# Compression of cached pages: copies of the next unit ahead of the second half's sums and activation, and the prompt units' turning split between the halves of layer 1

## The chip, the core and the metric

The kernel runs on one core of a Trainium2 chip. The metric is the device time of one execution in microseconds. TensorE does matmuls and transposes and writes them to PSUM; VectorE (DVE), ScalarE (ACT) and GpSimd (POOL) work element by element; SyncE (SP) and GpSimd issue the DMAs here. Each engine works through its own queue in order, and engines wait for each other by semaphores (`wait_ge`, `then_inc`).

## The reference, cut to what matters

One step of a hybrid decoder layer for a prompt of 1024 tokens and 8 sequences of the decode group with 2048 cached tokens each. The change touches only the compression of K and V of the compressed branch, which is done for the prompt (its new K and V rows) and for each decode sequence (its cached pages):

```python
def _compress(kraw, w1, b1, w2, b2, pe):
    ...
    ch = kp.reshape(B, n_ch, CMP_STRIDE, NSA_KV_HEADS, HEAD_DIM)
    w1r = w1.reshape(CMP_RATIO, CMP_STRIDE, HEAD_DIM, CMP_HIDDEN)
    parts = jnp.einsum('bnsgd,rsdh->rbngh', ch, w1r)
    n_cmp = n_ch - CMP_RATIO + 1
    h = parts[0, :, 0:n_cmp]
    for r in range(1, CMP_RATIO):
        h = h + parts[r, :, r:r + n_cmp]
    h = h + (pe.reshape(-1) @ w1) + b1
    out = jax.nn.gelu(h) @ w2 + b2
```

`CMP_STRIDE` is 16, `CMP_RATIO` 2, `HEAD_DIM` 64 with 2 KV heads, `CMP_HIDDEN` 256: a chunk of 16 rows goes through a layer of 256 hidden values with its neighbour, then through the activation and a second layer to 64.

## The kernel before

`compress_and_decode` holds the stage. Its work is cut into **units**, ten of them: unit 0 is the prompt's K, units 1 to 4 are K of two decode sequences each, unit 5 is the prompt's V, units 6 to 9 V of two sequences each. `units` has (which of K and V, pair, items); an **item** is one sequence's pages (or the prompt). `FIRST = (0, 5)` are the prompt units, with one item; all others have two.

TensorE runs, in its program order: the turning of unit 0, and then for each unit u the turning of unit u+1 (`transposes`), layer 1 of unit u (`layer1`), layer 2 of unit u-1 (`layer2`), and the second step of a set of ada rows (`late_back`). Turning a decode item is 16 transposes in four groups, each group into one PSUM bank; three banks rotate (`bank_free`: a group waits until the group three before it is copied). The prompt item has two groups. Layer 1 runs in two halves of 128 hidden values (`hh`), each into a bank of its own, for a decode unit with four sets of matmuls (L1114, L1116, L1121, L1123), since the chunks' halves are combined by sums and differences; for a prompt unit with 16 products (L1111). Ahead of one half of a decode unit stand 8 products for the ada vectors of a later stage (`late_rows`, L1081).

The other engines:

- `read_chunks` (L1209) copies the transposed groups out of PSUM into X, even groups on ScalarE, odd ones on VectorE, four instructions a group. X has two buffers, so copies of unit u wait for layer 1 of unit u-2.
- ScalarE: after the copies of the last item of unit u+1 it runs `gelu(u)`: for each half it waits for layer 1's half, copies the `middle` out of PSUM (L1261), perhaps the ada row (L1267), waits until VectorE has summed the half (`summed`) and applies the activation (L1270). Only then come the copies of unit u+2.
- VectorE: after the copies of the last item of unit u it forms the differences of both items (`first_difference`, L1304 to L1309), then `sums` of both halves of unit u-1 (L1328 to L1331, for a prompt unit L1321 and L1322), `late` (L1355: the ada addition, which waits for TensorE's `late_back`) and `out(u-2)` (L1342 or L1347: the result of layer 2).
- GpSimd: for each item it waits for the item's last transposes, loads the item that is four further on into the same of four raw buffers (L1011), and then forms another difference (`later_difference`, L1021), which waits for the item's copies.

A second half of layer 1 of unit u waits for `summed` of unit u-1's second half, and layer 2 of unit u-1 for its activation.

Of the kernel before, what the change touches and what calls it, by code (L numbers as in the profile page):

```python
# [18 lines left out]
ACT = mybir.ActivationFunctionType  # L19
# [589 lines left out]
FIRST = 4  # L609
# [261 lines left out]
def compress_and_decode(nc, a, o, m, PS, sem):  # L871
# [41 lines left out]
    with ExitStack() as st:  # L913
# [158 lines left out]
        def _(pe):  # L1072
# [18 lines left out]
            def layer1(u):  # L1091
# [9 lines left out]
                pe.wait_ge(pe_ready, which + 1)  # L1101
                for hh in range(2):
                    col = slice(P * hh, P * hh + P)
                    if u in late_at and hh == late_half(u):
                        late_rows(late_at.index(u))
                    if u:
# [56 lines left out]
                transposes(pe, items[k])  # L1163
            for u in range(NU):
                if u + 1 < NU:
                    for k in units[u + 1][2]:
                        transposes(pe, items[k])
                layer1(u)
                if u:
                    layer2(u - 1)  # L1170
                if u in late_at:
                    late_back(late_at.index(u))
# [77 lines left out]

        @block.scalar
        def _(act):
            def gelu(u):
                which = units[u][0]
                nb, c, nc_ = shape(u)
                for hh in range(2):
                    act.wait_ge(l1_done, 2 * u + hh + 1)
                    if u:
                        act.wait_ge(summed, 2 * (u - 1) + hh + 1)
                    if units[u][1] is not None:  # L1260
                        act.activation(m2[:, 2 * N3 * hh:2 * N3 * hh + 2 * N3], PS[:, 3, 0:2 * N3], ACT.Copy, scale=0.5).then_inc(m2_read, 1)  # L1261
                    if u in late_at and hh == late_half(u):
                        n = late_at.index(u)
                        act.wait_ge(wa_done, n + 1)
                        if n:
                            act.wait_ge(wa_back, n)
                        act.activation(arow[:, :], PS[:, 7, :], ACT.Copy).then_inc(wa_read, 1)  # L1267
                    act.wait_ge(summed, 2 * u + hh + 1)
                    act.wait_ge(hb_ready, 2 * which + hh + 1)
                    act.activation(H[:, u % 2, hh, 0:2 * nb * nc_], H[:, u % 2, hh, 0:2 * nb * nc_], ACT.Gelu_apprx_tanh,  # L1270
                                   bias=hb[:, which, hh:hh + 1]).then_inc(gelu_done, 1)
            u = 0
            for k in read_chunks(act, 0, even_read):
                if u + 1 < NU and k == units[u + 1][2][-1]:
                    gelu(u)
                    u += 1
            gelu(u)
            for k in read_keys(act, 0, even_read):
                if k == 1:
                    act.wait_ge(mins, 1)  # L1280
                    act.activation(SC, SC, ACT.Exp, bias=mn[:, 0:1], scale=-1.0, accum_out=sm[:, 0:1]).then_inc(exps, 1)
            decode.scalar(act)

        @block.vector
        def _(v):
# [71 lines left out]

            for k in read_chunks(v, 1, odd_read):
                u = items[k][0]
                if k == units[u][2][-1]:  # L1360
                    if u in FIRST:
                        bias_columns(units[u][0])
                    for x in units[u][2] if units[u][1] is not None else ():
                        first_difference(x)
                    if u:
                        for hh in range(2):
                            sums(u - 1, hh)
                        late(u - 1)
                    if u >= 2:
                        out(u - 2)  # L1370
            for hh in range(2):
                sums(NU - 1, hh)
            late(NU - 1)
# [2866 lines left out]
```

## Time and profile before

| | |
|---|---|
| median of 3 runs | 2225.09 us (2222.95 to 2227.34) |
| the profiled execution | 2226.52 us, span 2224.7 us |
| TensorE matmul busy | 2108.2 us, 95% of the span |
| VectorE, ScalarE, GpSimd busy | 1145.7, 793.7, 880.8 us |
| mean granted TensorE clock | 0.974 |
| compression | about 186 to 442 us of the span |

The page of the profile divides the span into 40 slices with the busy share of each engine; the compression is slices 4 to 8. A timeline row is a run of like instructions of one engine. "Idle before" names how long the engine had nothing running before the row and what ended it.

### The profile page before, as it was taken

What the parts mean: (1) busy time and instruction counts of PE and PEld (TensorE: products, weight loads), DVE (VectorE), ACT (ScalarE), POOL (GpSimd) and SP (SyncE); (2) the same over time, 40 slices, a digit from 0 to 9 for tenths busy, and PEclk for the clock granted to TensorE, in tenths of its full rate; (3) what the DMA queues carried; (4) which work ended last, traced back from release to release, by engine and by line L of the source; (5) the groups of instructions that cost most, each with busy time, mean ns of one, the idle gap of its engine ahead of it and who ended that gap; (6) DMA issues with size and microseconds to landing.
All of it is one profiled execution on the core that took longest, in us unless ns stands there. A gap on an engine that the chain in (4) does not pass through costs nothing. (4 is left out here: it accounts for less than half of the span.)

```text
span 2224.7 us, 38518 instructions
## 1 busy us (share of the span) xinstructions
PE 2108.2 (95%) x15606; PEld 1881.6 (85%) x15606; DVE 1145.7 (51%) x2132; ACT 793.7 (36%) x1654; POOL 880.8 (40%) x631
## 2 busy tenths in 40 slices
PE   5998999999999999998899999999999999999998
PEld 3997888856777689987899999678999999997886
DVE  5116545355676710258530054666865665654558
ACT  3203222234655611336412221234333333333553
POOL 2322121011111131211211223364388788776785
PEclk9999999988999999998899999999999999999999
DMA  7564534283100051100322130321244434357762
GB/s 267 193 214 160 183 121 152 92 304 139 32 32 11 1 143 39 39 9 3 99 76 57 47 125 4 117 95 41 86 162 151 139 132 166 129 182 284 266 226 105
DMA packets 152760, 268.23 MB, mean 121 GB/s; under 512 B 17817, under 2 KB 86348, under 8 KB 147975
## 3 DMA queue, kind: packets, MB, share of 16 engines
q1 hardware_dynamic: 144375, 222.70, 30.0%
q0 software_dynamic: 8208, 43.07, 5.5%
q8 instruction: 124, 2.03, 0.4%
q14 instruction: 53, 0.43, 0.1%
HBM read 211.93 MB, written 58.08 MB: 121 GB/s over the span
## 5 line engine op out<-in xcount | busy, mean ns | idle before, releaser
L3518 PE MATMUL PS<-down_parts 128*128 128x512 f32 x924 | 211.7, 390 | 1.1 <-DVE down_parts L4091 1.1
L3518 PEld LDWEIGHTS PS<-down_parts 128*128 128x128 f32 x924 | 173.1, 188 | 38.7 <-issue 2.0
L3475 PE MATMUL PS<-part_hi,w_ring 128*128 128x258 f32 x1152 | 192.3, 285 | 0.0
L3475 PEld LDWEIGHTS PS<-part_hi,w_ring 128*128 128x128 f32 x1152 | 162.1, 191 | 4.3 <-issue 4.3
L3475 PE MATMUL PS<-sum_blocks,w_ring 128*128 128x258 f32 x1296 | 161.6, 285 | 1.9 <-DVE out_sums L4041 1.9
L3475 PEld LDWEIGHTS PS<-sum_blocks,w_ring 128*128 128x128 f32 x1296 | 159.7, 192 | 2.1 <-DVE out_sums L4041 2.1
L651 POOL TENSOR_TENSOR w_merge_parts<-w_merge_raw,w_merge_parts 128x1024 fp32r<-128x1024 f32 x24 | 59.3, 2496 | 202.4 <-ACT w_merge_parts L644 183.6
L3867 POOL TENSOR_TENSOR down_parts<-down_raw,down_parts 128x512 fp32r<-128x512 f32 x71 | 118.5, 1686 | 43.2 <-ACT down_parts L3673 42.9
L2399 PE MATMUL PS<-h_hi,w_merge_parts 128*128 128x344 f32 x768 | 131.9, 324 | 0.0
L2399 PEld LDWEIGHTS PS<-h_hi,w_merge_parts 128*128 128x128 f32 x768 | 122.5, 189 | 3.1 <-issue 3.0
L1865 ACT ACTIVATE scores<-scores,mins_p 128x640 f32<-128x640 f32 (+5 forms) x192 | 112.5, 589 | 25.2 <-DVE mins_p L1907 24.4
L3673 ACT ACTIVATE down_parts<-down_raw 128x1024 fp32r<-128x1024 f32 x77 | 81.6, 1064 | 105.3 <-DMA down_raw<-w_down 59.0
L3475 PE MATMUL PS<-part_lo,w_ring 128*128 128x258 f32 x576 | 117.2, 285 | 0.0
L663 PE MATMUL PS<-h_hi,w_hg_parts 128*128 128x344 f32 x480 | 113.8, 320 | 0.0
L3824 POOL TENSOR_TENSOR w_ring<-w_raw,w_ring 128x512 fp32r<-128x512 f32 x72 | 99.0, 1377 | 35.5 <-ACT w_ring L3656 35.5
L4091 DVE TENSOR_TENSOR down_parts<-down_raw,down_parts 128x512 fp32r<-128x512 f32 x71 | 70.1, 999 | 68.4 <-ACT down_parts L3673 68.2
L1724 POOL TENSOR_TENSOR coef_T<-coef_T 128x128 f32<-128x128 f32 x32 | 14.6, 456 | 207.8 <-DVE coef_T L1951 207.8
L663 PE MATMUL PS<-h_hi,w_merge_parts 128*128 128x344 f32 x384 | 91.2, 320 | 1.6 <-DVE part_lo L2746 1.6
L1792 PE MATMUL PS<-ident,scores 128*128 128x128 f32 x592 | 83.1, 284 | 9.4 <-ACT PT L1840 6.1
L3824 POOL TENSOR_TENSOR w_ring<-w_sums,w_ring 128x512 fp32r<-128x512 f32 x54 | 74.1, 1372 | 42.3 <-ACT w_ring L3656 42.2
L3475 PEld LDWEIGHTS PS<-part_lo,w_ring 128*128 128x128 f32 x576 | 89.9, 191 | 0.0
L1907 DVE CUSTOM_DVE_ANT_0 scores<-PS,toeplitz 128x640 f32<-128x640 f32 (+15 forms) x160 | 77.3, 515 | 17.1 <-PE PS L1774 15.4
(617 smaller groups left out, 5182.9 us busy)
## 6 DMA issues: line engine op xcount, KB each, us to landing
down_raw<-act_blocks SPq DMA_DIRECT2D x77, 256.0 KB, 3.4
w_or_ada<-w_ada SPq DMA_DIRECT2D x8, 2048.0 KB
w_raw<-w_up SPq DMA_DIRECT2D x11, 1024.0 KB, 9.4
w_raw<-w_gate SPq DMA_DIRECT2D x11, 1024.0 KB, 6.7
w_down_rows<-w_down SPq DMA_DIRECT2D x11, 1024.0 KB, 7.3
w_down_blocks<-w_down_sums SPq DMA_DIRECT2D x11, 1024.0 KB, 8.7
down_raw<-w_down_blocks SPq DMA_DIRECT2D x44, 256.0 KB, 4.0
act_blocks<-act_sums SPq DMA_DIRECT2D x10, 1024.0 KB, 5.1
```

The source lines that it names most:

```text
L651: pool.tensor_tensor(r32(self.lo[:, u % 2, k, 0:cols]), self.raw[:, s, :, 0:cols], self.hi[:, u % 2, k, 0:cols], ALU.subtract).then_inc(se ...
L663: last = pe.matmul(out, r32(x), r32(y), start=k + i == 0, stop=k == tiles - 1 and i == 2)
L1792: last = pe.transpose(PS[:, 4 + G % 3, P * k:P * k + P], S[:, n % 2, g, at:at + P], ident[:, :])
L1865: act.activation(S[:, n % 2, g, c:c + cols], S[:, n % 2, g, c:c + cols], ACT.Exp, bias=mn[:, n % 2, x, g:g + 1], scale=-1.0, accum_out=sm[ ...
L1907: return v.tensor_tensor_reduce(S[:, n % 2, g, c:c + cols], src, bias, 1.0, 0.1 * BIG, ALU.add, ALU.min, mn[:, n % 2, x, g:g + 1])
L2399: last = pe.matmul(PS[:, e % RING, 0:W3], r32(left), r32(right), start=p == 0 and k == 0, stop=p == 2 and k == KD - 1)
L3475: last = pe.matmul(out[:, c, :], r32(w[:, k, :]), r32(h[:, k, QUART * c:QUART * c + QUART]), start=first and k + i == 0, stop=k == 3 and i ...
L3518: last = pe.matmul(PS[:, t, c], r32(s[:, x, P * (t % 4):P * (t % 4) + P]), r32(s[:, y, c]), start=first and i == 0, stop=last_j and i == 2 ...
L3673: act.activation(r32(slots[w % 12][:, 0:2, :]), draw[w % 4][:, :, :], ACT.Copy).then_inc(p_hi, 1)
L3824: pool.tensor_tensor(r32(ring[:, (q + 4) % 5, 1]), w_block(u, pos), ring[:, (q + 4) % 5, 0], ALU.subtract).then_inc(w_lo, 1)
L3867: pool.tensor_tensor(r32(s[:, 3, :]), d[:, 1, :], s[:, 1, :], ALU.subtract).then_inc(b_lo, 1)
L4091: v.tensor_tensor(r32(slots[w % 12][:, 2, :]), draw[w % 4][:, 0, :], slots[w % 12][:, 0, :], ALU.subtract).then_inc(a_lo, 1)
```

## The change

Three edits, all in `compress_and_decode`:

1. ScalarE's `gelu(u)` is cut into `middle(u, hh)` (the copies of the middle and of the ada row) and `gelu(u, hh)` (the activation). The second half's activation of unit u-2 now comes after the copies of the first item of unit u, where before it came ahead of all copies of unit u.
2. VectorE's `sums` of the second half of unit u-2 and `out(u-3)` likewise come after its copies of the first item of unit u. The first half's sums and `late` stay ahead of the copies.
3. On TensorE, the turning of the second item of units 1 and 6 stands between the two halves of layer 1 of the prompt units 0 and 5, where before it stood ahead of both.

```diff
@@ -1101,6 +1101,8 @@
                 pe.wait_ge(pe_ready, which + 1)
                 for hh in range(2):
                     col = slice(P * hh, P * hh + P)
+                    if hh and u in FIRST:
+                        transposes(pe, items[units[u + 1][2][1]])
                     if u in late_at and hh == late_half(u):
                         late_rows(late_at.index(u))
                     if u:
@@ -1163,7 +1165,7 @@
                 transposes(pe, items[k])
             for u in range(NU):
                 if u + 1 < NU:
-                    for k in units[u + 1][2]:
+                    for k in units[u + 1][2][:1 if u in FIRST else 2]:
                         transposes(pe, items[k])
                 layer1(u)
                 if u:
@@ -1250,31 +1252,40 @@
 
         @block.scalar
         def _(act):
-            def gelu(u):
+            def middle(u, hh):
+                act.wait_ge(l1_done, 2 * u + hh + 1)
+                if u:
+                    act.wait_ge(summed, 2 * (u - 1) + hh + 1)
+                if units[u][1] is not None:
+                    act.activation(m2[:, 2 * N3 * hh:2 * N3 * hh + 2 * N3], PS[:, 3, 0:2 * N3], ACT.Copy, scale=0.5).then_inc(m2_read, 1)
+                if u in late_at and hh == late_half(u):
+                    n = late_at.index(u)
+                    act.wait_ge(wa_done, n + 1)
+                    if n:
+                        act.wait_ge(wa_back, n)
+                    act.activation(arow[:, :], PS[:, 7, :], ACT.Copy).then_inc(wa_read, 1)
+
+            def gelu(u, hh):
                 which = units[u][0]
                 nb, c, nc_ = shape(u)
-                for hh in range(2):
-                    act.wait_ge(l1_done, 2 * u + hh + 1)
-                    if u:
-                        act.wait_ge(summed, 2 * (u - 1) + hh + 1)
-                    if units[u][1] is not None:
-                        act.activation(m2[:, 2 * N3 * hh:2 * N3 * hh + 2 * N3], PS[:, 3, 0:2 * N3], ACT.Copy, scale=0.5).then_inc(m2_read, 1)
-                    if u in late_at and hh == late_half(u):
-                        n = late_at.index(u)
-                        act.wait_ge(wa_done, n + 1)
-                        if n:
-                            act.wait_ge(wa_back, n)
-                        act.activation(arow[:, :], PS[:, 7, :], ACT.Copy).then_inc(wa_read, 1)
-                    act.wait_ge(summed, 2 * u + hh + 1)
-                    act.wait_ge(hb_ready, 2 * which + hh + 1)
-                    act.activation(H[:, u % 2, hh, 0:2 * nb * nc_], H[:, u % 2, hh, 0:2 * nb * nc_], ACT.Gelu_apprx_tanh,
-                                   bias=hb[:, which, hh:hh + 1]).then_inc(gelu_done, 1)
-            u = 0
+                act.wait_ge(summed, 2 * u + hh + 1)
+                act.wait_ge(hb_ready, 2 * which + hh + 1)
+                act.activation(H[:, u % 2, hh, 0:2 * nb * nc_], H[:, u % 2, hh, 0:2 * nb * nc_], ACT.Gelu_apprx_tanh,
+                               bias=hb[:, which, hh:hh + 1]).then_inc(gelu_done, 1)
+
             for k in read_chunks(act, 0, even_read):
-                if u + 1 < NU and k == units[u + 1][2][-1]:
-                    gelu(u)
-                    u += 1
-            gelu(u)
+                u = items[k][0]
+                if u >= 2 and k == units[u][2][0]:
+                    gelu(u - 2, 1)
+                if u and k == units[u][2][-1]:
+                    middle(u - 1, 0)
+                    gelu(u - 1, 0)
+                    middle(u - 1, 1)
+            gelu(NU - 2, 1)
+            middle(NU - 1, 0)
+            gelu(NU - 1, 0)
+            middle(NU - 1, 1)
+            gelu(NU - 1, 1)
             for k in read_keys(act, 0, even_read):
                 if k == 1:
                     act.wait_ge(mins, 1)
@@ -1357,17 +1368,20 @@
 
             for k in read_chunks(v, 1, odd_read):
                 u = items[k][0]
+                if u >= 2 and k == units[u][2][0]:
+                    sums(u - 2, 1)
+                    if u >= 3:
+                        out(u - 3)
                 if k == units[u][2][-1]:
                     if u in FIRST:
                         bias_columns(units[u][0])
                     for x in units[u][2] if units[u][1] is not None else ():
                         first_difference(x)
                     if u:
-                        for hh in range(2):
-                            sums(u - 1, hh)
+                        sums(u - 1, 0)
                         late(u - 1)
-                    if u >= 2:
-                        out(u - 2)
+            sums(NU - 2, 1)
+            out(NU - 3)
             for hh in range(2):
                 sums(NU - 1, hh)
             late(NU - 1)

```

On ScalarE, ahead of and in the turning of unit 3. Before: middle, ada row and activation of unit 1's second half, then copies of the first item.

```order
84 L1261 ACTIVATE middle<-PS 128x344 [waits cp_summed,cp_l1_done]
85 L1267 ACTIVATE ada_rows_late<-PS 128x512 [waits cp_wa_done]
86 L1270 ACTIVATE H<-H,hid_bias 128x508 [waits cp_hb_ready,cp_summed]
87 L1209 ACTIVATE XT<-PS 64x4x2x43 [waits cp_tr_done,cp_l1_done]
88 L1209 ACTIVATE XT<-PS 64x4x42
89 L1209 ACTIVATE XT<-PS 64x4x2x43
90 L1209 ACTIVATE XT<-PS 64x4x42
91 L1209 ACTIVATE XT<-PS 64x4x2x43 [waits cp_tr_done]
```

Now, the same place:

```order
84 L1260 ACTIVATE middle<-PS 128x344 [waits cp_summed,cp_l1_done]
85 L1266 ACTIVATE ada_rows_late<-PS 128x512 [waits cp_wa_done]
86 L1211 ACTIVATE XT<-PS 64x4x2x43 [waits cp_tr_done,cp_l1_done]
...
93 L1211 ACTIVATE XT<-PS 64x4x42
94 L1273 ACTIVATE H<-H,hid_bias 128x508 [waits cp_hb_ready,cp_summed]
95 L1211 ACTIVATE XT<-PS 64x4x2x43 [waits cp_tr_done,cp_l1_done]
96 L1211 ACTIVATE XT<-PS 64x4x42
```

The activation (line 1270 before, 1273 now) moved behind two groups of copies, and two more groups stand behind it.

On VectorE, in the turning of unit 4. Before, the second half's sums stand ahead of the ada addition:

```order
153 L1328 TENSOR_TENSOR middle<-middle 128x172 [waits cp_summed,cp_m2_read,cp_l2_done]
154 L1329 TENSOR_TENSOR H<-PS,middle 128x4x43 [waits cp_dve]
155 L1330 TENSOR_TENSOR H<-middle 128x4x42
156 L1331 TENSOR_TENSOR H<-middle,PS 128x4x42
157 L1355 TENSOR_TENSOR adaT<-PS,b_adaT 128x36 [waits cp_wa_back]
158 L1342 TENSOR_SCALAR kcT<-PS,b2k 128x254 [waits cp_l2_done]
159 L1209 COPY XT<-PS 64x4x2x43 [waits cp_tr_done,cp_l1_done]
```

Now they stand between the copies of the two items:

```order
153 L1366 TENSOR_TENSOR adaT<-PS,b_adaT 128x36 [waits cp_wa_back]
154 L1211 COPY XT<-PS 64x4x2x43 [waits cp_tr_done,cp_l1_done]
...
161 L1211 COPY XT<-PS 64x4x42
162 L1339 TENSOR_TENSOR middle<-middle 128x172 [waits cp_summed,cp_m2_read,cp_l2_done]
163 L1340 TENSOR_TENSOR H<-PS,middle 128x4x43 [waits cp_dve]
164 L1341 TENSOR_TENSOR H<-middle 128x4x42
165 L1342 TENSOR_TENSOR H<-middle,PS 128x4x42
166 L1353 TENSOR_SCALAR kcT<-PS,b2k 128x254 [waits cp_l2_done]
167 L1211 COPY XT<-PS 64x4x2x43 [waits cp_tr_done,cp_l1_done]
```

Sums (four instructions) and `out` moved behind two groups of copies.

On TensorE, at layer 1 of unit 0, as a piece of the difference (raw_572 is the second item of unit 1; a first line with [waits ...] and its "x15" or "x31" go together):

```order
+L1113 MATMUL PS<-XT,w_or_ada_570 128x130 [waits cp_w1_in0,cp_pe_ready,cp_odd_read,cp_even_read]
+L1113 MATMUL PS<-XT,w_or_ada_570 128x130 x15
 L1068 MATMUL PS<-ident,raw_572 128x128 [waits cp_odd_read,cp_raw_in1]
 L1068 MATMUL PS<-ident,raw_572 128x128 x3
...
-L1111 MATMUL PS<-XT,w_or_ada_570 128x130 [waits cp_w1_in0,cp_pe_ready,cp_odd_read,cp_even_read]
-L1111 MATMUL PS<-XT,w_or_ada_570 128x130 x31
+L1113 MATMUL PS<-XT,w_or_ada_570 128x130 x16
```

The first half's 16 products moved ahead of the turning of raw_572.

## Rows read from the trace of the kernel before

**Rows 1.** Windows: busy time (and instructions) of each engine, granted clock, DMA.

```profile
core 0: us, PE busy (x) PEld busy (x) DVE busy (x) ACT busy (x) POOL busy (x), PEclk, DMA share, GB/s
...
226.00:440.00 214.00, 204.19 (x1460) 182.82 (x1459) 102.41 (x225) 54.04 (x139) 38.43 (x32) 0.98 0.40 140
```

**Rows 2.** Timeline, turning of unit 4: start, duration, engine, line, operation, [idle before].

```profile
261.51 0.34 DVE L1328 TENSOR_TENSOR middle<-middle 128x172 f32<-128x172 f32 x1 [8.02 <-ACT middle L1261]
...
262.79 1.51 PE L1068 MATMUL PS<-ident,raw 128*128 128x128 f32 x12
262.79 0.72 ACT L1270 ACTIVATE H<-H,hid_bias 128x508 f32<-128x508 f32 x1 [1.37 <-DVE H L1331]
...
263.52 2.66 ACT L1209 ACTIVATE XT<-PS 64x344 f32<-64x344 f32 x8
263.96 6.28 DVE L1209 COPY XT<-PS 64x344 f32<-64x344 f32 x16 [0.41 <-PE PS L1068]
264.89 2.00 PE L1068 MATMUL PS<-ident,raw 128*128 128x128 f32 x12 [0.59 <-ACT XT L1209]
...
266.37 1.31 ACT L1209 ACTIVATE XT<-PS 64x344 f32<-64x344 f32 x4 [0.19 <-PE PS L1068]
...
267.26 1.36 POOL L1021 TENSOR_TENSOR XT<-XT 128x672 f32<-128x672 f32 x1 [0.49 <-DVE XT L1209]
...
268.32 1.92 PE L1081 MATMUL PS<-w_or_ada,cT 128*32 128x512 f32 x16
```

**Rows 3.** Timeline, turning of unit 9.

```profile
388.17 1.51 PE L1068 MATMUL PS<-ident,raw 128*128 128x128 f32 x12
...
388.90 2.66 ACT L1209 ACTIVATE XT<-PS 64x344 f32<-64x344 f32 x8 [0.57 <-PE PS L1068]
...
390.27 2.00 PE L1068 MATMUL PS<-ident,raw 128*128 128x128 f32 x12 [0.59 <-ACT XT L1209]
```

**Rows 4.** Timeline (two rows), then the tile `middle`: duration in ns min/median/max.

```profile
242.32 1.36 POOL L1021 TENSOR_TENSOR XT<-XT 128x672 f32<-128x672 f32 x1 [0.65 <-DVE XT L1209]
242.36 2.05 DVE L1307 TENSOR_TENSOR XT<-XT 128x688 f32<-128x688 f32 x1
...
L1328 DVE TENSOR_TENSOR middle<-middle x16: 336/337/2110, 222.0 to 440.7; 128x172 f32<-128x172 f32 x16
```

**Rows 5.** Windows with the granted clock, columns as in rows 1.

```profile
262.00:269.00 7.00, 6.03 (x48) 4.43 (x52) 6.19 (x18) 5.76 (x17) 2.53 (x3) 1.00 0.24 42
...
318.00:322.00 4.00, 3.90 (x20) 3.53 (x21) 2.86 (x9) 2.94 (x10) 2.30 (x3) 0.57 0.75 236
...
333.00:337.00 4.00, 2.86 (x22) 2.39 (x23) 3.21 (x9) 3.58 (x12) 1.98 (x2) 1.00 0.20 35
```

**Rows 6.** Timeline of TensorE, ada rows of unit 9.

```profile
417.33 3.61 PE L1081 MATMUL PS<-w_or_ada,cT 128*32 128x512 f32 x16 [0.38 <-DVE adaT L1355]
```

**Rows 7.** Timelines around the prompt units, 0 and 5.

```profile
191.62 3.44 PE L1068 MATMUL PS<-ident,raw 128*128 128x128 f32 x16 [1.78 <-DVE XT L1209]
...
194.86 7.65 PE L1111 MATMUL PS<-XT,w_or_ada 128*128 128x130 f32 x64
...
195.10 1.53 DVE L1209 COPY XT<-PS 64x344 f32<-64x344 f32 x4 [0.46 <-PE PS L1068]
...
202.62 0.88 DVE L1309 SCALAR_TENSOR_TENSOR XT<-XT 128x688 f32<-128x688 f32 x1
...
211.38 3.11 PE L1114 MATMUL PS<-XT,w_or_ada 128*128 128x172 f32 x16
...
318.10 4.16 PE L1068 MATMUL PS<-ident,raw 128*128 128x128 f32 x20 [2.19 <-ACT XT L1209]
...
330.08 0.88 DVE L1309 SCALAR_TENSOR_TENSOR XT<-XT 128x688 f32<-128x688 f32 x1
...
333.60 1.09 PE L1068 MATMUL PS<-ident,raw 128*128 128x128 f32 x8 [1.72 <-ACT XT L1209]
...
336.81 2.50 PE L1114 MATMUL PS<-XT,w_or_ada 128*128 128x172 f32 x16
```

## The prediction

> **What bounds the kernel now.** I read the engines' busy times in windows first: in 226 to 440 us, which is most of the compression, TensorE is busy for 204.19 of 214 us at a granted clock of 0.98 [rows 1]. So TensorE is the path of this stage; what is added to its idle time there is added to the end, and at most some 10 us can be won in this stretch. VectorE (102.41 us) and ScalarE (54.04 us) have much free time, but it lies inside layer 1, not where the idle time of TensorE is. Second, the timeline of one hand-over between units, all engines [rows 2]; third, another hand-over to see what gates the first copy [rows 3].
>
> I call T0 to T7 the eight groups of four transposes that turn one unit's two pages, and C0 to C7 their copies out of PSUM (even ones ScalarE, odd ones VectorE). Three PSUM banks rotate, so T3 waits for C0, T4 for C1, and so on: **T7 waits for C4**. Behind T7 on TensorE's queue stand the next ada rows and the layer 1 of the unit turned one step before.
>
> **What [rows 2] show.** When layer 1 has ended and ScalarE has copied the middle, VectorE sums the second half (first instruction 261.51) and ScalarE's activation starts 1.28 us later (262.79, 0.72 us long). TensorE is busy with layer 2 and the ada rows meanwhile: these sums lie wholly beside its work. T0 starts at 262.79, C0 at 263.52 (0.73 later), C1 at 263.96 (1.17 later), T3 at 264.89. The copies go at 2.66/2 = 1.33 us a group on ScalarE and at 6.28/4 = 1.57 on VectorE. C4 starts at 266.37, so T7 may start near 267.7, and the ada rows start at 268.32.
>
> **Part 1: copies ahead of the sums and the activation.** Can the first copies come earlier? In the turning of unit 9 the activation is out of the way early, and ScalarE waits 0.57 us for TensorE before C0; C0 again starts 0.73 after T0 (388.90 against 388.17), and T3 again 2.10 after T0 [rows 3], as in [rows 2]. So C0 and C1 are gated by the transposes, not by sums or activation, and moving these away wins nothing at the head of a turning. (The ada addition stays ahead of the copies, and it too waits for TensorE only.)
>
> Where they now stand they cost. After C1 and C3, at 263.96 + 2 x 1.57 = 267.10, VectorE does the four sums. ScalarE has finished C0 and C2 at 266.18 and waits for them with its activation at the queue's head; C4, C6 stand behind it. The activation starts 1.28 after 267.10, C4 at 267.10 + 1.28 + 0.72 = 269.10 in place of 266.37: **+2.73 us**, and T7, the ada rows and layer 1 move with it, since nothing else is ready on TensorE's queue.
>
> That is with the sums at their undisturbed speed. But GpSimd's difference for the first page begins when C3 is read, at 267.26, and lasts 1.36 us [rows 2]. An addition of VectorE with both inputs in SBUF that meets such a GpSimd operation takes 2.05 us, where one of the same size beside an idle GpSimd takes 0.88 [rows 4, 7]; and the sums' first instruction, at 337 ns mostly, has once taken 2110 [rows 4]. The third sum (both inputs in SBUF) would begin some 0.6 us after 267.10, and would be held until GpSimd ends at 268.6: about 1 us more. I take **+3.7 us** a turning; the ends are 2.7 (no collision) and 4.2 (the first sum is held and the later ones follow it). This takes place in four turnings, those of units 3, 4, 8 and 9, which all look alike: 4 x 3.7 = 14.8 us, between 10.9 and 16.8.
>
> The Trainium skill, "SBUF — State Buffer", section "Who interferes with whom", says that a VectorE instruction with two SBUF inputs contends with a GpSimd instruction that reads SBUF, and that who issues first holds the pair while the other blocks. By that rule the first sum, which starts before GpSimd does, holds GpSimd back by about 0.3 us and the third is held; the trace's 2.05 against 0.88 agrees with it. By a reading in which the first sum loses, the term is 4.2.
>
> GpSimd's page loads wait for T3 and T7 and are issued up to 5 us later; their pages are turned two units on (some 50 us), so they cost nothing. SyncE's loads of the ada weights wait for the ada rows and move with them. If such a load were late after all, TensorE would wait for a DMA, which it doesn't do now in [rows 2].
>
> Unit 5's turning has two groups and nothing waits for its copies (the ada rows follow at once): 0 us. The new alternation of Copy and activation on ScalarE reloads no table: in [rows 2] the activation stands between copies, without a load.
>
> **The clock.** TensorE's granted clock falls from 1.00 to 0.50 (2.4 to 1.2 GHz) after some idle stretches: after the 2.19 us of idle time before 318.10 the next 4 us have 0.57 on average; after the 1.72 us before 333.60 they keep 1.00 [rows 5, 7]. One fall at 417.3 makes sixteen ada matmuls take 3.61 us in place of 1.92 [rows 2, 6]: 1.7 us lost where TensorE has work queued. The new idle stretch ahead of T7 is 3.7 us, longer than either of those, and what follows is exactly the ada rows and layer 1. I take one such fall in each of the four turnings: 4 x 1.7 = **6.8 us**; the ends are 0 and, if some falls double, 10.
>
> The Trainium skill, "TensorE: Matmul & The Clock Gate", section "Part 4: PE-mode transpose", says that transposes don't count as busy for the clock as matmuls do. By that rule the clock would drop at each turning already, the change could add no fall, and the sum would be 18.0 us, as in rival B. The trace disagrees: 262 to 269, a whole turning, has 1.00 [rows 5].
>
> **Part 2: prompt units' turning split.** Half of layer 1 of unit 0 (7.65/2 = 3.8 us) moves into the idle time before 191.62 (1.78 us) [rows 7]. TensorE finishes this layer earlier by about 2 us. But VectorE is the late one here: the second page's last copy ended at 196.63 and now ends at some 198.0, since its transposes start 3.8 us after 189.84; the two differences behind it (to 203.50, 6.8 us without a gap [rows 7]) and the first sum end 1 to 1.4 us later. ScalarE's queue now has the first half's activation, with the table load, ahead of unit 2's C0, and waits for that sum, so this C0 is late too, by some 0.6 us. Then sum and activation of the second half (0.35 + 0.35) again stand between C3 and C4. By the same reckoning C3 ends at 210.2, C4 at 212.3, and layer 1 of unit 1 starts at 212.8 instead of 211.38 [rows 7]: **+1.4 us** (0 to 2). What TensorE wins early it waits away before T3.
>
> Units 5 to 7: before 318.10 TensorE is idle for 2.19 us, because sums of up to 2110 ns in place of 337, held up by GpSimd, kept both copiers [rows 4, 7]. This is a real gain: copies now start with the transposes (C0 near 315.1), half of layer 1 fills the time in which sums and activation run, and layer 1 of unit 5 ends some 2.2 us earlier. But VectorE's differences, which end at 330.96 (330.08 + 0.88) [rows 7], end no earlier; copies of unit 7 begin at 331.5 to 332 as before, then sum and activation stand between C3 and C4, and layer 1 of unit 6 starts near 338.1 instead of 336.81: +1.3, and with the longer idle time ahead of T3 (3.6 us) a clock fall that costs about 0.5. **+1.8 us** (-2 to +3).
>
> **The sum.** 14.8 + 6.8 + 1.4 + 1.8 = 24.8 us. The later stages start later by as much and are otherwise the same. The profiled execution has its own time of 2226.52 us (span 2224.7), 1.4 above the median of 2225.09; 24.8 on the median gives **2250 us**, +1.1%.
>
> **Rivals.**
> A. The forecast, stall with falls of the clock: 2246 to 2257. Chance 0.50.
> B. The stall without falls: 2225.1 + 14.8 + 3.2 = 2243, between 2235 and 2246. For it: one idle stretch of 1.72 us had none. Chance 0.28.
> C. Faster: C4 isn't late, because ScalarE reaches it before the sums matter, and only the fills at units 0 and 6 count: 1.78 + 2.19 + some of the four heads' 0.59 us [rows 2, 3], at most 6 us: 2219. It decides from the point at which the activation ends before T4 is read, 266.37; but C3 ends at 267.10 and the activation needs the sums behind it. So only a wrong reading of the queues' order gives this. Chance 0.08.
> D. No difference: the change moves waits only, the stalls before T7 replace gains at units 0 and 6 of equal size. It needs the turnings to cost under 1 us each. Chance 0.09.
> E. More than 2257: falls that last longer, or the sums held up twice. Chance 0.05.
>
> A and B are both slower; a measurement of this kernel tells about 0.2% (4.4 us) from no change. Slower 0.83, within 0.2% 0.09, faster 0.08. The range from 2235 (10.9 for the turnings, nothing for the clock, -1 for the prompt units) to 2257 (16.8 + 10 + 5) holds A and B, 0.78 or a little more.
>
> **What would show it.** Right: in the four turnings ScalarE idle for 2 to 3 us before the activation, waiting for the last sum; TensorE's wait for ScalarE's copies (by [rows 2, 3] 0.59 a head) grown by 3 to 4 us each, just before the last group of transposes; clock rows of 0.5 behind them; T3 still 2.10 after T0; sums at 1.3 us, with one of them near 1.2 us long. Wrong: if the last transposes follow as before at 1.9 us after C3's middle, the turnings are free, and the time is C's or D's. If the third sum keeps 0.37 us, the term is 2.7 instead of 3.7. If the stretch from unit 6 to unit 7 is shorter by over 1 us, VectorE isn't the late one there.

## The result, and the profile after

| | before | after |
|---|---|---|
| median | 2225.68 us (4 runs, 2222.95 to 2227.34) | 2252.12 us (4 runs, 2245.58 to 2253.26) |
| profiled execution | 2226.52 us, span 2224.7 | 2245.58 us, span 2243.8 |
| compression, unit 1's T0 to the turning behind layer 1 of unit 9 | 186.46 to 442.12: 255.7 us | 184.77 to 466.66: 281.9 us |

The ratio is 1.0117, interval 1.0097 to 1.0137: slower, by 26 us at the median; 24.8 us were forecast (2250, between 2235 and 2257). (A ratio here is an estimate from all runs of both kernels and can differ by 0.1% from the quotient of the medians.) The profiled execution of after is the fastest of its four. Its span is only 19.1 us longer, though its compression is 26.2 us longer; some 7 us were made up outside this stage, 1.7 of them ahead of it, in code that the change doesn't touch. What that is wasn't tried. Below I compare mostly the compression alone. Each kernel has one trace; for all ten kernels the change in its compression agrees with the change of the median within some 4 us.

The same hand-over as in [rows 2], the turning of unit 4, in the timeline of after (start, duration, engine, line, operation, [idle before]). The lines are 2 to 11 higher than before.

```profile
268.40 1.51 PE L1068 MATMUL PS<-ident,raw 128*128 128x128 f32 x12
269.13 2.66 ACT L1211 ACTIVATE XT<-PS 64x344 f32<-64x344 f32 x8 [2.10 <-PE PS L1068]
269.57 3.15 DVE L1211 COPY XT<-PS 64x344 f32<-64x344 f32 x8 [0.80 <-PE PS L1068]
270.50 2.00 PE L1068 MATMUL PS<-ident,raw 128*128 128x128 f32 x12 [0.59 <-ACT XT L1211]
...
272.76 0.34 DVE L1339 TENSOR_TENSOR middle<-middle 128x172 f32<-128x172 f32 x1
...
272.87 1.44 POOL L1021 TENSOR_TENSOR XT<-XT 128x672 f32<-128x672 f32 x1 [0.49 <-DVE XT L1211]
...
273.40 1.16 DVE L1341 TENSOR_TENSOR H<-middle 128x168 f32<-128x168 f32 x1
...
274.83 0.72 ACT L1273 ACTIVATE H<-H,hid_bias 128x508 f32<-128x508 f32 x1 [3.04 <-DVE H L1342]
...
275.57 2.64 ACT L1211 ACTIVATE XT<-PS 64x344 f32<-64x344 f32 x8
276.93 1.11 PE L1068 MATMUL PS<-ident,raw 128*128 128x128 f32 x4 [3.49 <-ACT XT L1211]
```

The head of the turning is as before: C0 0.73 us after T0, C1 1.17, T3 2.10. ScalarE now stands idle for 2.10 us ahead of C0, so having it free early won nothing. Then the sums stand behind C3; the third (L1341) takes 1.16 us instead of some 0.37 because GpSimd's L1021 runs from 272.87; ScalarE stands for 3.04 us, and C4 starts at 275.57, 7.17 after T0, where it was 3.58 in [rows 2]. TensorE is idle for 3.49 us ahead of T7. TensorE's waits for ScalarE's copies in the whole stage show in the view of waits (waiter, what it waited for, us in total, times, longest), in 180 to 470 us of after:

```profile
PE PS L1068 <- ACT XT L1211: 32.5, 16, 6.8
```

and in the same stretch of the kernel before:

```profile
PE PS L1068 <- ACT XT L1209: 11.1, 10, 3.5
```

Behind it the clock has fallen (timeline of TensorE, and windows with the granted clock in the third column from the end, all of after; 1.00 is the level of 2.4 GHz, 0.50 that of 1.2):

```profile
277.97 3.64 PE L1081 MATMUL PS<-w_or_ada,cT 128*32 128x512 f32 x16
...
278.00:282.00 4.00, 4.00 (x19) 1.02 (x19) 3.79 (x7) 0.21 (x2) 2.29 (x2) 0.50 0.45 141
...
418.00:422.00 4.00, 4.00 (x21) 1.03 (x20) 3.48 (x6) 0.96 (x4) 2.30 (x2) 0.57 0.43 129
```

The sixteen ada matmuls took 1.92 us in [rows 2]; they take 3.64, 3.64, 3.58 and 3.47 us in the turnings of units 3, 4, 8 and 9. The prompt units' places, and the ada rows of unit 9, in the timeline of TensorE of after:

```profile
206.34 3.86 PE L1068 MATMUL PS<-ident,raw 128*128 128x128 f32 x16 [6.80 <-ACT XT L1211]
...
345.70 3.85 PE L1068 MATMUL PS<-ident,raw 128*128 128x128 f32 x16 [4.45 <-ACT XT L1211]
...
351.50 3.57 PE L1116 MATMUL PS<-XT,w_or_ada 128*128 128x172 f32 x16
...
443.56 1.92 PE L1081 MATMUL PS<-w_or_ada,cT 128*32 128x512 f32 x16 [0.38 <-DVE adaT L1366]
```

TensorE now waits 6.80 us ahead of unit 2's T3 and 4.45 ahead of unit 7's (before 1.72, [rows 7]), and behind the latter the transposes and the first products of layer 1 run at half clock. Ahead of unit 2's T3 the kernel before waited for 3.51 us:

```profile
207.33 1.10 PE L1068 MATMUL PS<-ident,raw 128*128 128x128 f32 x8 [3.51 <-ACT XT L1209]
```

### The profile page after: what moved, and what is told of

It is laid out like the page before. It is cut to its first block and busy times, and to the rows that moved or that the text cites. A ratio compares the mean times of both kernels' runs of the same rounds, so it can differ in the third digit from the quotient of the medians.

```text
span 2243.8 us, 38518 instructions
## 1 busy us (share of the span) xinstructions
PE 2103.7 (94%) x15606; PEld 1872.7 (83%) x15606; DVE 1144.2 (51%) x2132; ACT 793.7 (35%) x1654; POOL 879.6 (39%) x631
## 3 DMA queue, kind: packets, MB, share of 16 engines
q1 hardware_dynamic: 144375, 222.70, 29.8%
## 5 line engine op out<-in xcount | busy, mean ns | idle before, releaser
L1879 ACT ACTIVATE scores<-scores,mins_p 128x640 f32<-128x640 f32 (+5 forms) x192 | 112.4, 588 | 25.4 <-DVE mins_p L1921 24.6
L1068 PE MATMUL PS<-ident,raw 128*128 128x128 f32 x384 | 59.1, 303 | 34.2 <-ACT XT L1211 32.5
```

Of the source, the lines that this page charges most:

```text
L1879: act.activation(S[:, n % 2, g, c:c + cols], S[:, n % 2, g, c:c + cols], ACT.Exp, bias=mn[:, n % 2, x, g:g + 1], scale=-1.0, accum_out=sm[ ...
```

## The experiments

For each kernel I measured three stretches of its TensorE timeline: a turning from T0 to the second set of products of the layer 1 behind it (9.82 us before in each of units 3, 4, 8 and 9), unit 1's T0 to the same set of unit 1 (27.86 before), unit 6's T0 to that of unit 6 (24.75 before), and the whole compression as above. "Second set" means its start, the first matmul with 168 columns. The trace shows a product as two matmuls (the eight ada products are x16, here also called sixteen ada matmuls) and a transpose as one.

| kernel | turnings 3, 4, 8, 9 (us) | unit 1 on | unit 6 on | compression | median | ratio (interval) |
|---|---|---|---|---|---|---|
| before | 9.8 each | 27.9 | 24.8 | 255.7 | 2225.6 to 2226.5 | 1 |
| after | 15.7, 15.8, 15.1, 15.0 | 29.3 | 28.9 | 281.9 | 2252.12 | 1.0117 (1.0097 to 1.0137) |
| e1_order_alone | 15.1, 15.9, 15.0, 15.1 | 29.8 | 29.4 | 282.4 | 2251.99 | 1.0121 (1.0096 to 1.0147) |
| e2_split_alone | 9.8 each | 28.7 | 28.9 | 258.9 | 2228.26 | 1.0008 (0.9998 to 1.0019) |
| e3_sums_back | 10.3 each | 28.1 | 25.7 | 256.8 | 2227.39 | 1.0007 (0.9992 to 1.0023) |
| e4_pool_later | 12.6, 12.6, 12.6, 14.3 | 29.3 | 27.4 | 270.9 | 2242.08 | 1.0077 (1.0054 to 1.0099) |
| e5_filled_wait | 15.1 each | 30.9 | 29.2 | 282.4 | 2248.18 | 1.0105 (1.0088 to 1.0122) |
| e5b_filled_short | 13.4 each | 29.3 | 29.2 | 274.3 | 2241.22 | 1.0077 (1.0056 to 1.0097) |
| e6_woven | 8.3 each | 27.3 | 25.6 | 248.2 | 2218.82 | 0.9967 (0.9955 to 0.998) |
| e7_prompt_late | 8.3 each | 24.3 | 25.0 | 244.6 | 2213.91 | 0.9955 (0.9937 to 0.9972) |
| e8_unit6 | 8.3 each | 24.3 | 24.6 | 244.1 | 2211.96 | 0.9946 (0.9928 to 0.9965) |

Two things in this table come and go without the code, and differences below 2 us between single traces are to be read with them in mind. The ada rows of unit 9 took 3.61 us in the trace of the kernel before ([rows 6]) and 1.92 in all ten others, whatever their edits, so every compression compared with before's has 1.7 us in its favour that I can't put down to an edit. And after, e4_pool_later, e5_filled_wait and e5b_filled_short have the same TensorE, ScalarE and VectorE code up to unit 2, with 29.3, 29.3, 30.9 and 29.3 us for "unit 1 on": the granted clock was 0.50 for 7.3 us around the wait of 6.80 in after and for 10.3 us around the same wait in e5_filled_wait.

### e1_order_alone: the new order without the split

The changed kernel with the turning of units 1 and 6 undivided:

```diff
-                    if hh and u in FIRST:
-                        transposes(pe, items[units[u + 1][2][1]])
...
-                    for k in units[u + 1][2][:1 if u in FIRST else 2]:
+                    for k in units[u + 1][2]:
```

> The new order on ScalarE and VectorE alone; the turning of units 1 and 6 isn't split. My theory (the second half's sums between C3 and C4 make ScalarE's activation and so C4 and T7 late, and the clock falls behind the wait): the four turnings of units 3, 4, 8 and 9 cost as in the changed kernel, 5.2 to 6 us each, 22 us together, with 3.5 us of idle time ahead of T7 and 0.5 of the clock after it; with 1 to 3 us at the prompt units the time is 2226 + 24 = 2250 us (2246 to 2254). Rival (the split turning costs most of it): within 10 us of before, 2236 or less.

2251.99 us, and the four turnings are the same as after within 0.7 us (TensorE, unit 4; the last two rows are unit 6):

```profile
277.32 1.11 PE L1068 MATMUL PS<-ident,raw 128*128 128x128 f32 x4 [3.49 <-ACT XT L1209]
278.36 3.64 PE L1081 MATMUL PS<-w_or_ada,cT 128*32 128x512 f32 x16
...
335.04 1.12 PE L1068 MATMUL PS<-ident,raw 128*128 128x128 f32 x4 [3.50 <-ACT XT L1209]
335.95 9.61 PE L1111 MATMUL PS<-XT,w_or_ada 128*128 128x130 f32 x64
```

The order of copies, sums and activation carries the loss. With it, the split makes no difference that one trace can tell (281.9 us of compression with it, 282.4 without). But the loss at units 6 and 7 has another form here: without the split, unit 6's turning has the same stall ahead of T7, 3.50 us with a fall of the clock behind it, a fifth one. In the changed kernel half of layer 1 of unit 5 stands between T3 and the second page's transposes, and the wait ahead of T7 is 0.93 us.

### e2_split_alone: the split without the new order

The piece that e1_order_alone took out, put by itself into the kernel before: only TensorE's turning of units 1 and 6 is split.

> The split turning of units 1 and 6 alone; ScalarE and VectorE in the old order. My theory: the four turnings are as before (0.59 us ahead of T3, 5.5 us from T0 to the ada rows); at unit 0 layer 1 ends 2 us earlier, but VectorE's differences end 1 us later and unit 2's C0 with them, so +1 us; at unit 5 nothing is won, for the copies still stand behind the sums: 2226 to 2229 us. Rival (the split costs most of it): 2240 or more. Rival (the split wins by itself what the order gives back): 2222 or less.

2228.26 us, as forecast (the interval, 0.9998 to 1.0019, holds no difference too), and the four turnings are untouched. But in the trace the compression is 3.2 us longer: 0.8 more at unit 1, 4.1 more at units 6 and 7, where I had expected nothing, and the 1.7 less at unit 9's ada rows. TensorE's timeline at unit 2 and at unit 7:

```profile
210.22 4.64 PE L1068 MATMUL PS<-ident,raw 128*128 128x128 f32 x20 [7.09 <-ACT XT L1211]
...
338.36 4.71 PE L1068 MATMUL PS<-ident,raw 128*128 128x128 f32 x20 [4.74 <-ACT XT L1211]
```

The split alone lets TensorE run ahead (idle 4.74 us instead of 1.72 ahead of unit 7's T3), and VectorE's chain gets longer: the second page's transposes now stand behind half of layer 1, so the differences behind its copies end 18.6 us after unit 6's T0 instead of 16.6, and unit 7's T3 starts 21.3 us after it instead of 19.2. That is 2.1 of the 4.1 us. The other 2.0 lie behind this T3, where the granted clock was 0.50 (337.4 to 344.4). The wait of 2.19 us ahead of unit 6's T3, which in the kernel before had a fall behind it ([rows 5, 7]), is there unchanged, and this time the clock stayed at 1.00.

### e3_sums_back: which of the two moved steps costs

The changed kernel, VectorE in the old order:

```diff
-                if u >= 2 and k == units[u][2][0]:
-                    sums(u - 2, 1)
-                    if u >= 3:
-                        out(u - 3)
...
-                        sums(u - 1, 0)
+                        for hh in range(2):
+                            sums(u - 1, hh)
```

> The changed kernel, but VectorE's sums of both halves and its second-layer result ahead of the copies again; ScalarE's second activation stays between C2 and C4. My theory: it is the wait for the sums, not the activation's place, that costs. The activation (0.72 us) then runs at once after C2, C4 is late by 0.5 us at most, no fall of the clock in the four turnings: 4 x 0.5 = 2 us, with 1 to 4 us at the prompt units 2229 us (2226 to 2233). Rival (ScalarE's order by itself costs): 5 us a turning as in the changed kernel, 2245 or more.

2227.39 us, 1.0007: no difference from before that can be measured. TensorE at unit 4, and at unit 7:

```profile
269.12 0.66 PE L1068 MATMUL PS<-ident,raw 128*128 128x128 f32 x4 [0.34 <-ACT XT L1211]
269.70 1.92 PE L1081 MATMUL PS<-w_or_ada,cT 128*32 128x512 f32 x16
...
335.18 4.08 PE L1068 MATMUL PS<-ident,raw 128*128 128x128 f32 x20 [4.46 <-ACT XT L1211]
339.10 2.50 PE L1116 MATMUL PS<-XT,w_or_ada 128*128 128x172 f32 x16
```

The activation between C2 and C4 costs 0.34 us ahead of T7 and 0.43 a turning, and the ada rows keep their 1.92 us. So ScalarE's order is nearly harmless; what costs is that the sums it waits for come behind C3. (The compression is 1.1 us longer than before's; with unit 9's ada rows as slow as there it would be 2.8. The sums' move with the activation left ahead of all copies wasn't run.) At unit 7 the wait is as long as in after, 4.46 against 4.45 us, but the clock was at 0.50 only from 335.0 to 338.5, before layer 1 starts, and the stretch from unit 6 on is only 0.9 us longer than before.

### e4_pool_later: the collision with GpSimd

The changed kernel; GpSimd waits with the first page's difference until the sums are done:

```diff
                 pool.wait_ge(odd_read, read_to(it))
+                if i == 0 and u >= 2:
+                    pool.wait_ge(summed, 2 * (u - 2) + 2)
```

> The changed kernel, with GpSimd's difference of a unit's first page held until the second half's sums are done. My theory: the third sum takes 0.37 us in place of 1.16, so C4 and T7 come 0.8 to 1 us earlier in each of the four turnings (2.5 to 2.7 us of idle time ahead of T7 in place of 3.49), with the falls of the clock still there: 3 to 4 us less than the changed kernel, 2248 us. If the falls go too, 2242. Rival (the collision with GpSimd isn't on the path): idle time ahead of T7 of 3.49 us as before, 2252.

2242.08 us. VectorE's third sum and TensorE behind it at unit 4, and TensorE's ada rows at unit 9:

```profile
270.23 0.37 DVE L1343 TENSOR_TENSOR H<-middle 128x168 f32<-128x168 f32 x1
...
272.98 0.66 PE L1070 MATMUL PS<-ident,raw 128*128 128x128 f32 x4 [2.70 <-ACT XT L1213]
273.56 1.92 PE L1083 MATMUL PS<-w_or_ada,cT 128*32 128x512 f32 x16
...
407.17 3.19 PE L1083 MATMUL PS<-w_or_ada,cT 128*32 128x512 f32 x16
```

The sum takes 0.37 us, and the wait ahead of T7 is 2.70 us, 0.79 less than 3.49: the collision is on the path with its full length. The compression is 11 us shorter than after, though, not 3 to 4: with 2.70 us of idle time the clock fell in only one of the four turnings (unit 9), and unit 6's stretch is 1.6 us shorter. The time is that of the case "if the falls go too". So 0.8 us of collision was worth 2.4 to 3.2 us in a turning where it also decided the clock.

### e5_filled_wait and e5b_filled_short: the clock by itself

The changed kernel with products between T6 and T7 of the four turnings that nobody reads (24, then 15 of them), in the bank that the next layer 1 overwrites:

```diff
+                if q == 3 and filler:
+                    pe.wait_ge(summed, 2 * (u - 2) + 1)
+                    for _ in range(filler):
+                        pe.matmul(PS[:, 4, 0:128], ident[:, :], ident[:, :], start=True, stop=True)
```

> The changed kernel, with 24 extra products of 128 columns (some 3.1 us, results never read) on TensorE between T6 and T7 in the four turnings, where it now waits 3.49 us. They give no useful work; they only keep it busy. My theory: T7 starts when it does now (8.5 us after T0), but the clock stays at 1.00, so sixteen ada products take 1.92 us in place of 3.5 to 3.64: 4 x 1.8 = 7 us less than the changed kernel, 2245 us. Rival (the falls don't come from the idle time): ada products at 3.5 us still, 2252 us or more.

2248.18 us, ratio 1.0105 (1.0088 to 1.0122), compression 282.4 us. I had sized the product wrongly: 24 took 5.5 us, not 3.1, and T7 came 1.7 us late. That ate the gain; the clock did stay full (TensorE, unit 3):

```profile
249.69 0.60 PE L1072 MATMUL PS<-ident,raw 128*128 128x128 f32 x4
250.22 1.92 PE L1085 MATMUL PS<-w_or_ada,cT 128*32 128x512 f32 x16
```

> As e5_filled_wait with 15 extra products instead of 24. There each product took 0.22 us, so that 24 of them (5.2 us) outlasted the wait (3.49 us) and T7 came 10.2 us after T0 instead of 8.5; the clock stayed full, and the one made up for the other. 15 products take 3.3 us and fit in. My theory: T7 8.5 us after T0 as in the changed kernel, clock at 1.00, sixteen ada products in 1.92 us: 1.7 to 1.9 us less in each of the four turnings, 7 us less than the changed kernel, 2245 us, and compression (unit 1's T0 to the end of layer 1 of unit 9) some 7 us shorter than the 281.9 of the changed kernel. Rival (what follows is late for another reason): 2252 us.

2241.22 us, 4 us less than expected, though the compression came out as expected. TensorE at unit 3:

```profile
239.31 3.51 PE L1068 MATMUL PS<-ident 128*128 128x128 f32 x30
...
242.99 0.66 PE L1072 MATMUL PS<-ident,raw 128*128 128x128 f32 x4 [0.17 <-ACT XT L1215]
243.58 1.92 PE L1085 MATMUL PS<-w_or_ada,cT 128*32 128x512 f32 x16
```

T7 comes 8.55 us after T0 as in after, but all four turnings take 13.4 us instead of 15.0 to 15.8, and the compression 7.6 us less. That is the clock's share, shown by doing useless work in the wait: 1.6 to 2.4 us a turning. It goes with how long the clock stayed at 0.50 in after: 7 us in the turnings of units 3 and 4 (2.3 us lost each), 3.5 us in those of units 8 and 9 (1.6 each). What is left over before, 3.6 us a turning, is the late C4.

### e6_woven: useful work in the gaps

The kernel before; the ada rows' eight products, which stand behind the turning, are split, four ahead of T3 and four ahead of T6 (in the turnings of units 3, 4, 8 and 9):

```diff
-                    for k in units[u + 1][2]:
-                        transposes(pe, items[k])
+                    for i, k in enumerate(units[u + 1][2]):
+                        ahead = (3 - 1 * i, lambda: late_rows(late_at.index(u), (i,))) if woven(u) else None
+                        transposes(pe, items[k], ahead)
```

> The kernel before, with the ada rows' 8 products (1.92 us, which stand behind a turning) split and put into the turnings of units 3, 4, 8 and 9: four ahead of T3, four ahead of T6. My theory (TensorE's gaps in a turning come from the rate of the copies and of the rotating banks, and nothing but other work of TensorE can fill them): the gaps of 0.59 and 0.28 and those between T3 and T7 go, T0 to layer 1 takes 6.0 us in place of 7.38, 4 x 1.4 = 5.5 us won, 2220 us (ratio 0.9975). Rival (the copies are the bound of the whole turning, so layer 1 starts no earlier): 2225.5.

2218.82 us, 0.9967 (0.9955 to 0.998): faster than before, and 1.2 us less than the forecast. TensorE's turning of unit 4 has no idle time left:

```profile
258.86 1.51 PE L1070 MATMUL PS<-ident,raw 128*128 128x128 f32 x12
260.30 1.06 PE L1084 MATMUL PS<-w_or_ada,cT 128*32 128x512 f32 x8
261.30 1.67 PE L1070 MATMUL PS<-ident,raw 128*128 128x128 f32 x12
262.89 1.07 PE L1084 MATMUL PS<-w_or_ada,cT 128*32 128x512 f32 x8
263.89 1.09 PE L1070 MATMUL PS<-ident,raw 128*128 128x128 f32 x8
```

9.82 us became 8.30 in all four, 6.1 us together; the rest of the 7.5 us of the compression is the 1.7 at unit 9's ada rows, which isn't this edit's, and small ones of both signs.

### e7_prompt_late: what the prompt units wait for

As e6_woven; ScalarE's activations of units 0 and 5 stand behind all copies of units 2 and 7, and VectorE is left as it was:

```diff
-                    gelu(u)
+                    if u not in FIRST:
+                        if u and u - 1 in FIRST:
+                            gelu(u - 1)
+                        gelu(u)
```

> As e6_woven, and in addition ScalarE's activations of the prompt units 0 and 5 stand behind all copies of units 2 and 7, so that C0 doesn't wait for VectorE's differences. My theory: C0 of unit 2 starts 0.73 us after T0, TensorE's wait of 3.51 us ahead of T3 becomes shorter by 1.5 us (then T4 waits for VectorE's C1), the same with 0.5 us at unit 7: 2 us less than e6_woven, 2218 us. Rival (VectorE's late copies bound these two turnings anyway): the same as e6_woven.

2213.91 us (2210.04 to 2222.28; e6_woven had 2212.80 to 2223.52), 0.9955 (0.9937 to 0.9972). The times of the two overlap; what tells them apart is the trace, whose compression is 3.6 us shorter, where 2 were expected. TensorE at unit 2:

```profile
201.64 0.66 PE L1070 MATMUL PS<-ident,raw 128*128 128x128 f32 x4 [0.60 <-ACT XT L1217]
204.15 1.06 PE L1070 MATMUL PS<-ident,raw 128*128 128x128 f32 x8 [1.85 <-DVE XT L1217]
```

T3 waits 0.60 us, T4 then 1.85 for VectorE's C1, and layer 1 of unit 1 starts 3 us earlier than in e6_woven. Part of that may be the clock: it stayed at 1.00 here, and in e6_woven it was at 0.50 from 206.2 to 209.7, behind a wait of 4.57 us. Here too an activation is put off behind copies, and here it wins: its sums were late already (behind VectorE's differences), at unit 0 a load of ScalarE's function table (1.28 us) stands ahead of it and moves with it, and it now stands behind the last copy, where nobody waits behind it.

### e8_unit6: the change's own idea where there was a wait

As e7_prompt_late; at unit 6 alone, the sums and the activation of unit 4's second half stand behind all copies:

```diff
                 if k == units[u][2][-1]:
+                    if u == FIRST[1] + 1:
+                        sums(u - 2, 1)
+                        out(u - 3)
```

(with ScalarE's activation moved to match, and the same steps taken out of their old place).

> As e7_prompt_late, and in unit 6's turning alone the second half's sums and activation of unit 4 stand behind all copies (not between them, as in the change). My theory: the wait of 2.19 us ahead of T3 there becomes 0.59, T7 isn't held since nothing stands between C3 and C4, layer 1 of unit 5 starts 1.3 to 1.6 us earlier, and VectorE's differences, which unit 7's copies wait for, end 1 to 2 us earlier: 1.5 to 2 us less than e7_prompt_late, 2212 us. Rival (VectorE is the bound from there to unit 7, whatever the order): 2214.

2211.96 us, 0.9946 (0.9928 to 0.9965). The compression is 0.5 us shorter than e7_prompt_late's, not 1.5 to 2. The wait ahead of T3 fell to 0.59 us, as expected, but came back between the halves of layer 1 of unit 5, which wait for the same sums:

```profile
317.54 3.84 PE L1118 MATMUL PS<-XT,w_or_ada 128*128 128x130 f32 x32 [2.28 <-DVE H L1352]
```

The sums again met GpSimd (the first took 1.16, the third 2.21 us). Between e7_prompt_late and e8_unit6 neither the medians nor 0.5 us of compression tell.

## Why the prediction was right, point by point

- **TensorE is the path of the stage.** Right: the compression grew by 26.2 us in the profiled execution and the median by 26.4.
- **Nothing is won at the head of a turning.** Right: C0, C1 and T3 stand 0.73, 1.17 and 2.10 us after T0, as in [rows 2, 3].
- **The stall before T7, +3.7 us.** C4 came 7.17 us after T0 against 3.58, +3.59. The third sum took 1.16 us for 0.37, 0.8 more where about 1 was reckoned; the first wasn't held (0.34), and GpSimd's operation grew by 0.08 us, to 1.44, not by 0.3. (The undisturbed 0.88 us that the prediction sets against 2.05 is, in [rows 7], a row of another operation, L1309; additions of L1307 without a GpSimd operation beside them take 0.88 too.) e3_sums_back shows that the sums' place is the cause, given ScalarE's new order; e4_pool_later the collision's 0.79 us. Of the two ends given, 2.73 without the collision came out in e4_pool_later as 2.8 (12.62 against 9.82), in the three turnings without a fall.
- **One fall of the clock in each of the four, 1.7 us each.** Right: four of four, in e1_order_alone too. e5b_filled_short measures it as 1.6 to 2.4 us (T7 itself and the first products of layer 1 are also slow, which I had left out). The four turnings cost 5.87, 5.96, 5.25 and 5.22 us, 22.3 in all; 21.6 were forecast. The ground for it was thinner than it looked: the fall behind 2.19 us of idle time, on which the prediction rests ([rows 5, 7]), didn't come behind the same wait in e2_split_alone, e6_woven and e7_prompt_late. The nearer row in the trace of before was the wait of 3.51 us at 207.33, with a fall behind it.
- **Unit 1 to 2, +1.4.** Measured 29.30 against 27.86, +1.44, but that is in part luck. Layer 1 of unit 1 started 2.05 us later, not 1.4 (26.97 us after unit 1's T0 against 24.92), and 0.6 us came back because its first set of products ran at full clock, where in the kernel before it still ran at half (3.11 us for 2.50). With the same code the stretch took 30.9 us in e5_filled_wait.
- **Units 5 to 7, +1.8: too small.** Layer 1 of unit 5 did end 2.2 us earlier after T0 of unit 6 (12.73 against 14.94), and VectorE's differences ended 0.8 us later. But the stretch grew by 4.2 us. The larger part of the miss is the clock fall of "about 0.5": TensorE was idle for 4.45 us, and the clock was at 0.50 from within this wait to within layer 1 of unit 6 (343.3 to 353.8), so that its first sixteen matmuls took 3.57 us instead of 2.50. In e4_pool_later, after a wait of 4.76 us, it was at 0.50 only from 339.3 to 342.8, and the stretch is 1.6 us shorter. The smaller part is the delay of layer 1: even with that shorter fall it started 2.6 us later than before in e4_pool_later, where 1.3 and 0.5 for a fall were reckoned. The split isn't needed for a loss of this size: the stretch is 4.1 us longer with the split alone (e2_split_alone) and 4.7 us with the order alone (e1_order_alone), each in its own way.
- **Not foreseen:** the fall that the kernel before had at unit 9's ada rows ([rows 6]) wasn't there after (1.92 us for 3.61), -1.7 us. 22.3 + 1.4 + 4.2 - 1.7 = 26.2. No other trace has that fall, so this term is chance as far as the runs show, and it made up for most of what units 5 to 7 lacked. That the sum came within 2 us is therefore partly luck; that the four turnings did isn't.

The rivals: B (no falls) is refuted by the clock rows. C and D would have needed C4 in time. E's falls that last longer did come, 7 and 10.5 us at 0.50 in after against about 3.5 us in the kernel before, but they cost too little to pass 2257.

## What to carry to other kernels

When a producer's buffers rotate, look where in the rotation a step is put. Here a step between C3 and C4 that had to wait (the sums and what waits for them) was on TensorE's path with its full length; ahead of C0 it was free as long as TensorE was still busy; behind the last copy it was a gain at the prompt units (e7_prompt_late), and at unit 6 most of the gain came back as another wait for the same sums (e8_unit6). Before clearing the way for a step that waits, look whether it starts at a fixed distance after what it waits for, as C0 does 0.73 us after T0; then the work in front of it isn't what holds it. What helped against TensorE's waits for copies was other work of its own in the gaps (e6_woven). And before a fall of the clock is counted for or against an edit, look whether it comes in other traces with the same code there.

## What the runs showed of the hardware

A wait is worth more than its length where it takes the clock with it. In the same place of the same program, 3.49 us of idle time went with a granted clock of 0.50 in eight of eight turnings, and 2.70 us in one of four; a fall cost 1.6 to 2.4 us, so shortening the wait by 0.79 us won up to 3.2. Over the compression of all eleven traces, all 24 waits of 3.35 us or more had the clock at 0.50, from within the wait or at most 1.8 us behind its end, and of the 17 waits of 1.72 to 2.70 us six did; the same wait of 2.19 us ahead of unit 6's T3 had a fall in the kernel before and none in three others. The clock then stayed at 0.50 for some 3.5 to 10.5 us, and differently behind equal waits: behind 4.45 us in after for 10.5, behind 4.46 us in e3_sums_back for 3.5. Products that nobody reads, put into the wait, saved 7.6 us of 282.

A VectorE addition with two inputs in SBUF that began 0.1 us before GpSimd's operation wasn't held by it (0.34 us) while the one after next was (1.16). The Trainium skill, "SBUF — State Buffer", section "Who interferes with whom", says that the order of issue decides which of the two blocks, and these rows agree with it. The order of starts in a trace doesn't always tell it: in the kernel before, VectorE's L1309 at 326.17 took 2.15 us instead of 0.88, although GpSimd's L1021 starts only at 326.20, and the third sum of 2.21 us in e8_unit6 started 0.61 us ahead of GpSimd's L1021.
